# A streamed two-layer decoder trunk: memory transposed as it lands, and a dozen hand-offs in a new order

## The chip, the cores and the metric

One core of one Trainium2 chip. The metric is the device time of one execution in microseconds; less is better. The trace comes from one profiled execution of the same program. The engines are called as in the profile: PE (TensorE), PEld (its weight loads), DVE (VectorE), ACT (ScalarE), POOL (GpSimd) and SP (SyncE, which here only issues DMAs).

## The reference

`x` is 256 tokens by 1024 channels, `mem` 256 rows by 1024, fp32. For each of 2 layers:

```python
h = rms_norm(x);  z = h @ W_in            # one combined projection
x += W_o(sum_i sigmoid(gate_i) * lift_i(branch_i))   # attention, spatial gating, pooling
x += memory_xattn(rms_norm(x), rms_norm(mem))        # 4 heads of 128, 256 memory rows
x += peer_ffn(rms_norm(x))

def memory_xattn(h, mem_h, wq, wk, wv, q_norm, k_norm, wo):
    q = rms_norm((h @ wq) per head, q_norm); k = rms_norm((mem_h @ wk) per head, k_norm)
    p = softmax(q @ k.T * XA_HEAD_DIM ** -0.5);  return (p @ (mem_h @ wv)) @ wo

def peer_ffn(h, wq, keys1, keys2, u_tab, v_tab):     # 8 heads, top 16 of 128*128 experts
    # scores of two half queries against 128 keys each, top 16 of each, top 16 of the 256 sums,
    # softmax weights w;  out = sum over chosen experts e of w_e * gelu(h . u_tab[e]) * v_tab[e]
```

The kernel does not gather experts. It computes gelu(h . U) for all 16384, multiplies by a weight that is zero for those not chosen, and multiplies by the whole of V.

## The kernel before, in words

All weights pass through the core once, as a **stream** of 128x512 pieces in the order in which they are used. A layer has its projection pieces (`PROJ` of them, in the blocks `mem_k, mem_v, z_q ... z_m0-5, lift_*, out0/1, xq, xo0/1, pq0/1`), then 256 pieces of U and 256 of V (two per key, 128 keys). SP loads two pieces per transfer (L427) into a ring `raw` of four. For fp32-like precision each piece is split: ACT writes the rounded part `w_hi` (`hi_piece`, L499), POOL the rest `w_lo = raw - w_hi` (L453), each into one of 4 slots. PE multiplies hi by hi, lo by hi and hi by lo, (`take`, L817 to L819, six 128x512 matmuls a piece; U pieces twelve 128x256 ones, L1079 to L1081; V pieces six, L1108 to L1110) and frees the slot (`used`). ACT's `hi(n)` writes the next n pieces' high parts, 4 ahead of PE; where it stands between ACT's other steps is written by hand, and so is every order in the program: each engine has one instruction list, and `wait(name)`/`step(..., name)` pair them by semaphores. POOL has only the low parts. Products go into 4 PSUM banks `acc` (two blocks of two in turn), transposes and small products into 4 banks `aux`, whose users and order are the table `USES`.

A block's input rows are transposed by PE (L752 memory, L779 all else), read from `aux` by ACT as `h_hi` (L470, L527) and by DVE as `h_lo` (L1171). Products leave through `read_block` on DVE, which scales by 1/rms (L1207).

- **Start.** ACT issues memory, constants, columns and X; SP streams from the beginning. ACT squares the two memory tiles with a sum, takes the root, DVE normalizes them (L1136), PE transposes, ACT and DVE make hi and lo; then the layer loop, whose head is ACT's `hi(SLOTS)`. The same memory preparation for layer 1 lies inside layer 0's V stage (`NORM_AT`, `MEM_AT`).
- **Mixer.** `mix_T0..3` are the transposed rows of the normalized x; ACT writes six pieces' high parts only after `mix_T3`. The attention units (16, each 2 heads) take exponentials on ACT (L601). When `hi` passes the last piece of gate block `z_m{m}`, ACT reads that block at once (`read_gates`, L518), between two units.
- **Memory attention** (L1489 to L1530 on DVE, L636 on ACT, L779, L987, L1007 on PE). The query block is read for both tiles, squared and reduced, then the root. Four units (tile, pair of heads): scores, maximum, exponential, transposes, values, with a ring of two.
- **PEER start.** `ff_T0/1`, eight pieces of pq0, `ff_T2/3`, pq1, then transposes of the queries (`pq_T`) and their 32 score matmuls (L1033), then the U loop over 128 keys.
- **One-hot weights.** During the first half of U, DVE does the top-k (L1577 among it). At key 52 (`EXP_AT`) ACT takes the softmax; at 56 (`SLOTS_AT`) PE transposes the slots; DVE splits them and makes the operands `hot_b` (L1612), `hot_a` (L1620), `hot_w` (L1626) for 8 tokens a step; from key 64 PE multiplies them (L1047, 24 small matmuls) between keys, to the middle of V.
- **V.** PE starts the four `acc` banks with matmuls by zeros, adds all V pieces, closes them by zeros. `eg` is the weighted activation (ACT L696 hi, DVE L1642 lo).
- **Layer end.** DVE adds `acc` to X (L1710), one 128x1024 op per token tile; at the end of the program SP writes X to DRAM in one transfer.

## Time and profile before

| | us |
|---|---|
| median of 3 runs | 2285.96 (2284.37 to 2287.23) |
| the profiled execution's own time | 2284.8 |
| its span in the trace | 2283.0 |
| PE busy | 2194.2 (96%) |
| PEld busy | 1936.4 (85%) |
| POOL busy | 1751.1 (77%) |
| DVE busy | 1400.0 (61%) |
| ACT busy | 1169.1 (51%) |
| streamed | 672 transfers of 512 KB, mean 161 GB/s with all others |

The page gives the chain of work that ended last as 91% PE, 3% DVE, 3% issue, 1% ACT and 1% POOL. In its row of 40 slices PE stands at 9 tenths or more in all but five: the first has 6, the sixth (memory attention and PEER start of layer 0) 7, the slice of the memory attention of layer 1 and one in its U stage have 8, the last 8. A time in a row of the trace counts from the span's start. An idle time in square brackets stands before the group and names what ended it; busy times of matmuls overlap, so that the pitch from start to start is what one costs.

### The profile page before, as it was taken

How to read it: one execution, taken by the hardware profiler on the slowest of the kernel's cores; microseconds unless marked ns; L12 is line 12 of the kernel's file. 1: busy time of each engine (PE TensorE's matmuls, PEld its weight loads, DVE VectorE, ACT ScalarE, POOL GpSimd, SP SyncE). 2: the span in 40 equal slices, each digit the busy share in tenths (PEclk: the TensorE clock that was granted, in tenths of full speed). 3: DMA queues.
4: the chain of work that ended last, by engine and by line, in shares of the span. 5: the costliest groups of instructions: out<-in, count | busy, mean ns of one | idle time of the engine just before them, and what ended most of it. 6: DMA issues, size and time to landing. Idle time of an engine off the chain costs nothing.

```text
span 2283.0 us, 51302 instructions
## 1 busy us (share of the span) xinstructions
PE 2194.2 (96%) x15526; PEld 1936.4 (85%) x15530; DVE 1400.0 (61%) x2291; ACT 1169.1 (51%) x2273; POOL 1751.1 (77%) x1316
## 2 busy tenths in 40 slices
PE   6999979999999999999999998899999999999998
PEld 5887868999999888888878777699999998888887
DVE  4644547994666788734346455489756667886333
ACT  5445654555444455556553555645554444455564
POOL 5745846998777788888885557579987777888886
PEclk9999999999999999999998999999999999999999
DMA  6423423445444444455563234335544444445554
GB/s 243 157 93 110 158 98 136 173 167 182 157 164 157 157 168 169 168 203 187 191 237 130 102 111 166 106 136 174 174 167 164 157 162 159 165 165 191 187 193 147
DMA packets 100517, 367.12 MB, mean 161 GB/s; under 512 B 11472, under 2 KB 11984, under 8 KB 100176
## 3 DMA queue, kind: packets, MB, share of 16 engines
q1 hardware_dynamic: 97040, 353.41, 44.6%
q10 hardware_dynamic: 3392, 12.66, 1.5%
q8 instruction: 42, 0.69, 0.1%
q14 instruction: 43, 0.35, 0.1%
HBM read 364.98 MB, written 1.05 MB: 160 GB/s over the span
## 4 chain that ended last, share of the span: by engine, by line
PE 91%; DVE 3%; issue 3%; ACT 1%; POOL 1%; DVEq 0%; POOLq 0%; ACTq 0%
PE acc L1079 11%; PE acc L1080 10%; PE acc L1081 10%; PE acc L1108 10%; PE acc L1110 10%; PE acc L1109 10%; PE acc L817 6%; PE acc L819 6%; PE acc L818 6%; PE aux L1047 4%; PE aux L779 2%; POOL w_lo L453 1%; PE aux L930 1%; PE aux L865 1%; DVE h_lo L1171 1%
## 5 line engine op out<-in xcount | busy, mean ns | idle before, releaser
L453 POOL TENSOR_TENSOR w_lo<-raw,w_hi 128x512 fp32r<-128x512 f32 x1312 | 1750.9, 1350 | 519.6 <-ACT w_hi L499 424.9
L499 ACT ACTIVATE w_hi<-raw 128x512 fp32r<-128x512 f32 x1344 | 843.3, 630 | 809.3 <-PE acc L1081 424.1
L1079 PE MATMUL acc<-h_hi,w_hi 128*128 128x256 f32 x2048 | 587.0, 287 | 9.7 <-POOL w_lo L453 9.7
L1080 PE MATMUL acc<-h_lo,w_hi 128*128 128x256 f32 x2048 | 579.3, 283 | 0.0
L1081 PE MATMUL acc<-h_hi,w_lo 128*128 128x256 f32 x2048 | 579.0, 283 | 0.0
L1108 PE MATMUL acc<-w_hi,eg 128*128 128x512 f32 x1024 | 406.2, 397 | 1.2 <-DVE eg L1642 1.2
L1079 PEld LDWEIGHTS acc<-h_hi,w_hi 128*128 128x128 f32 x2048 | 392.6, 192 | 12.6 <-POOL w_lo L453 12.5
L1110 PE MATMUL acc<-w_hi,eg 128*128 128x512 f32 x1024 | 399.6, 390 | 0.0
L1109 PE MATMUL acc<-w_lo,eg 128*128 128x512 f32 x1024 | 398.7, 389 | 0.0
L1080 PEld LDWEIGHTS acc<-h_lo,w_hi 128*128 128x128 f32 x2048 | 393.0, 192 | 0.1
L1081 PEld LDWEIGHTS acc<-h_hi,w_lo 128*128 128x128 f32 x2048 | 392.7, 192 | 0.0
L1642 DVE TENSOR_TENSOR eg<-big,eg 128x256 fp32r<-128x256 f32 x256 | 188.5, 736 | 228.7 <-ACT eg L696 227.7
L1612 DVE TENSOR_TENSOR hot_b<-aux,sel 128x1024 bf16<-128x1024 f32 x128 | 156.8, 1225 | 206.4 <-PE aux L1047 186.0
L819 PE MATMUL acc<-w_hi,h_lo 128*128 128x512 f32 x640 | 252.3, 394 | 0.0
L1110 PEld LDWEIGHTS acc<-w_hi,eg 128*128 128x128 f32 x1024 | 192.2, 188 | 41.5
L1108 PEld LDWEIGHTS acc<-w_hi,eg 128*128 128x128 f32 x1024 | 192.4, 188 | 39.7 <-POOL w_lo L453 2.0
L1109 PEld LDWEIGHTS acc<-w_lo,eg 128*128 128x128 f32 x1024 | 192.6, 188 | 38.3
L696 ACT ACTIVATE eg<-big 128x256 fp32r (+1 forms) x256 | 106.8, 418 | 206.3 <-PE acc L1110 206.0
L817 PE MATMUL acc<-w_hi,h_hi 128*128 128x512 f32 x416 | 172.3, 414 | 12.8 <-POOL w_lo L453 5.8
L818 PE MATMUL acc<-w_lo,h_hi 128*128 128x512 f32 x416 | 163.2, 392 | 0.0
L819 PEld LDWEIGHTS acc<-w_hi,h_lo 128*128 128x128 f32 x640 | 121.0, 189 | 26.5
L1626 DVE TENSOR_TENSOR hot_w<-sel,aux 128x1536 bf16<-128x1536 bf16 x64 | 112.3, 1754 | 8.9 <-DVE sel L1620 1.8
(235 smaller groups left out, 2336.8 us busy)
## 6 DMA issues: line engine op xcount, KB each, us to landing
raw<-stream_dram SPq DMA_DIRECT2D x672, 512.0 KB, 3.2
big<-parb_dram ACTq DMA_DIRECT2D x2, 2128.0 KB, 10.1
big<-mem_dram ACTq DMA_DIRECT2D x3, 1024.0 KB, 5.3
big<-pm_dram ACTq DMA_DIRECT2D x2, 768.0 KB, 15.1
big<-parr_dram ACTq DMA_DIRECT2D x2, 640.0 KB, 12.1
X<-x_dram ACTq DMA_DIRECT2D x1, 1024.0 KB, 12.0
out_dram<-X SPq DMA_DIRECT2D x1, 1024.0 KB, 4.0
big<-lnrow_dram ACTq DMA_DIRECT2D x2, 256.0 KB, 13.2
```

Source lines behind the costliest of these rows:

```text
L453: nc.gpsimd.tensor_tensor(w_lo[:, k % SLOTS, :], raw[:, k // PER_CHUNK, k % PER_CHUNK, :], w_hi[:, k % SLOTS, :].bitcast(F32), ALU.subtrac ...
L499: nc.scalar.activation(w_hi[:, k % SLOTS, :], raw[:, (k // PER_CHUNK) % RAW, k % PER_CHUNK, :], ACT.Copy).then_inc(hi_ready, 1)
L817: pe_.matmul(dst, r_hi[:, kt, ts], w_hi[:, slot, :], start=(k == 0), stop=False)
L818: pe_.matmul(dst, r_hi[:, kt, ts], w_lo[:, slot, :], start=False, stop=False)
L819: ins = pe_.matmul(dst, r_lo[:, kt, ts], w_hi[:, slot, :], start=False, stop=(k == depth - 1))
L1079: pe_.matmul(acc[:, q, 0:S], wh, h_hi[:, kt, :], start=(kt == 0), stop=False)
L1080: pe_.matmul(acc[:, q, 0:S], wh, h_lo[:, kt, :], start=False, stop=False)
L1081: ins = pe_.matmul(acc[:, q, 0:S], w_lo[:, r % SLOTS, k * P:(k + 1) * P], h_hi[:, kt, :], start=False, stop=(kt == KD - 1))
L1108: pe_.matmul(dst, eg[:, q % 2, 0, ts], w_hi[:, slot, :], start=False, stop=False)
L1109: pe_.matmul(dst, eg[:, q % 2, 0, ts], w_lo[:, slot, :], start=False, stop=False)
L1110: ins = pe_.matmul(dst, eg[:, q % 2, 1, ts], w_hi[:, slot, :], start=False, stop=False)
L1642: V.tensor_tensor(eg[:, q % 2, 1, :], src, eg[:, q % 2, 0, :].bitcast(F32), ALU.subtract).then_inc(sig["eg_ready"].sem, 1)
```

## The change

- **A, start.** The constants' and memory's transfers go first, and SP holds the stream back until memory, columns and constants have landed. The memory rows are transposed raw; their 1/rms is applied when `mem_k` and `mem_v` are read. DVE takes their squares once per program (`msq`), ACT one root per layer for memory and X together (`factors`). The rows are not normalized in the V stage either. ACT's first four pieces alternate with the memory's high parts.
- **B, mixer.** ACT's squares of X alternate with pieces; `hi(2)` stands ahead of `mix_T3`, `hi(4)` behind.
- **C, gates.** A gate block that comes due within the units is read after the next unit's exponentials.
- **D, memory attention.** Per token tile: rows read by DVE, squares by ACT, reduction by DVE, transposes by PE. The Exp table is asked for ahead of the scores. Rings and banks for all four units; all four score products first.
- **E, PEER start.** `ff_T0..3` at once; keys 0 and 1 of U between the readings of pq0 and pq1, keys 2 and 3 between the queries' transposes and their scores (`first_keys`); the U loop starts at key 4. `EXP_AT, SLOTS_AT` become 56, 60.
- **F, one-hots.** All one-hot operands are bf16 with an innermost pair `[.., 2]`; iota and weight parts lie in PSUM as bf16 pairs, where they were fp32.
- **G, V.** No matmuls by zeros: the first and last pieces carry the start and stop flags. PE does the first two weight steps at the head of V and stays two ahead.
- **H, layer boundary.** ACT writes the next layer's first four high parts at the end of a layer, ahead of its loop branch; SP loads two more chunks at the very end for it.
- **I, layer end.** X is added in half columns, the first half after the last but one piece; output in two transfers, one per token tile.

```diff
+USES += [(f"xs{u}", u) for u in range(len(XUNITS))] + [(f"xp_T{u}", u) for u in range(len(XUNITS))]
+USES += [("xo_0", 0), ("xo_1", 2), ("xo_T0", 1), ("xo_T1", 3)]
 USES += [(f"{r}_T{i}", (i + 2) % 4) for r in ("fu", "ff") for i in range(4)]
-USES += [(f"pq_T{i}", i) for i in range(4)]
...
-EXP_AT, SLOTS_AT = 52, 56
+EXP_AT, SLOTS_AT = 56, 60
...
-        iota_b = sb("iota_b", [P, P], BF16)
+        slot_a = sb("slot_a", [P, S, 2], BF16)
         hot_b = sb("hot_b", [P, G_TOK, KEYS], BF16)
         hot_w0 = sb("hot_w0", [P, G_TOK, PARTS, HALF], BF16)
...
+        xring = region("xring", 2048, 4, 2, MEM)
+        xsquare = region("xring", 1024, T, COL)
+        xpT = region("xpT", 2048, 4, 4, P)
...
-        slots = topv.bitcast(BF16)
-        slot_a, slot_b = slots[:, 0:S], slots[:, S:2 * S]
+        slot_b = topv.bitcast(BF16).rearrange("p (t n) -> p t n", n=2)
         slot_w = sel[:, 512:768]
-        slot_parts = sel[:, 768:1280].bitcast(BF16)[:, 0:PARTS * S].rearrange("p (c t) -> p c t", c=PARTS)
+        slot_parts = hot_w0.rearrange("p t c a -> p (t c a)").rearrange("p (t c n) -> p t c n", c=PARTS, n=2)
...
+        parts_ps = upper[:, 0:PARTS * S].bitcast(BF16).rearrange("p (t c n) -> p t c n", c=PARTS, n=2)
+        rest_ps = upper[:, PARTS * S:PARTS * S + P // 2].bitcast(BF16).rearrange("p (a n) -> p a n", n=2)
...
+            sp.wait_ge(sig["mem_in"].sem, 32)
+            sp.wait_ge(const_in, 16)
...
-            sp.wait_ge(sig["layer_free"].sem, sig["layer_free"].value(DEPTH, 0))
-            sp.dma_start(out.rearrange("(t p) d -> p t d", p=P), X[:]).then_inc(out_done, 16)
-            sp.wait_ge(out_done, 16)
+            for r in range(SLOTS // PER_CHUNK):
+                sp.wait_ge(lo_ready, DEPTH * PIECES + (r + 1) * PER_CHUNK)
+                sp.dma_start(raw[:, r], stream[r:r + 1].rearrange("o p (k c) -> p (o k) c", c=COL)).then_inc(chunk_in[r], 16)
+
+            for t in range(T):
+                sp.wait_ge(sig["layer_free"].sem, sig["layer_free"].value(DEPTH, t - 1))
+                sp.dma_start(out[t * P:(t + 1) * P, :], X[:, t, :]).then_inc(out_done, 16)
+            sp.wait_ge(out_done, T * 16)
...
             for i in range(4):
+                hi_piece(i, 16, i + 1)
                 memory_hi(first, i)
...
+                                due.append(m)
+                                if not late:
+                                    read_gates(due.pop())
...
-                hi(SLOTS)
                 for t in range(T):
                     a.wait("layer_free", t - 1)
                     if t == 0:
                         act.wait_ge(x_in, 16)
                     a.step(nc.scalar.activation(junk[:, t, :], X[:, t, :], ACT.Square, accum_out=ssx[:, t:t + 1]),
                            "x_sq" if t else None)
-                hi(2)
-                root(ssx, "x_mean", "x_sqrt", 1)
+                    hi(1)
+                root(factors, "x_mean", "x_sqrt", 1)
                 hi(1)
...
                 hi_T("mix_T2", 4, 2, C_MIX + 4)
+                hi(2)
                 a.wait_pieces(16)
                 hi_T("mix_T3", 6, 2, C_MIX + 6)
-                hi(6)
+                hi(4)
...
+                    if due:
+                        read_gates(due.pop())
+                    hi(2, u < len(UNITS) - 1)
...
+                    if t == 0:
+                        a.wait("xq_rows")
+                    else:
+                        a.wait_block("xq")
+                    a.step(nc.scalar.activation(xsquare[:, t, :], xqt[:, t, :], ACT.Square), "xq_square")
...
+                a.step(nc.scalar.activation(st[:, 96:97], ident[:, 0:1], ACT.Exp))
...
-                for n in range(2):
-                    hi((3, 8)[n])
-                    for i in (2 * n, 2 * n + 1):
-                        hi_T(f"ff_T{i}", 2 * i, 2, C_FFN + 2 * i)
+                hi(3)
+                for i in range(2):
+                    hi_T(f"ff_T{i}", 2 * i, 2, C_FFN + 2 * i)
+                hi(6)
+                a.wait_pieces(LAST["pq1"] - 2)
+                hi_T("ff_T2", 4, 2, C_FFN + 4)
+                hi(2)
+                a.wait_pieces(LAST["pq1"])
+                hi_T("ff_T3", 6, 2, C_FFN + 6)
                 assert done[0] == PROJ + SLOTS
...
+                hi(SLOTS)
...
+                e.wait_block("mem_v")
+                for u in range(len(XUNITS)):
+                    e.wait_drained(f"xq_T{XUNITS[u][0]}")
+                    xscores(u)
+                xprobs(0)
+                for u in range(len(XUNITS)):
+                    if u + 1 < len(XUNITS):
+                        xprobs(u + 1)
...
+                rows_T([f"ff_T{i}" for i in range(4)], xn)
                 take(8)
...
                 e.wait_block("pq0")
+                first_keys(0)
                 e.wait_block("pq1")
                 rows_T([f"pq_T{i}" for i in range(4)], pq)
+                first_keys(2)
...
+                for k0, k1 in ((4, SLOTS_AT), (SLOTS_AT, HALF), (HALF, KEYS)):
...
-                pe_.wait_ge(zero_set, 1)
-                pe_.wait_ge(sig["u_out"].sem, layer * KEYS + (KEYS + 4))
-                for q in range(4):
-                    pe_.matmul(acc[:, q, :], zeros[:], zeros[:, 0:1].broadcast_to((P, COL)), start=True, stop=False)
...
+                weights_step(0, 0, 1)
+                weights_step(0, 1, 1)
+                for r in range(8):
+                    if r < 2:
+                        pe_.wait_ge(sig["u_out"].sem, layer * KEYS + (KEYS + 3 + r))
+                    value_piece(0, 0, r, start=r < 2)
...
+                            if k0 == 4 and r % 4 == 0:
+                                weights_step(i, r // 4, 1, 2)
...
-            first.step(V.tensor_scalar(ssm, ssm, 1.0 / D, EPS, ALU.mult, ALU.add))
-            dve.sem_inc(mem_mean, 1)
-            dve.wait_ge(mem_sqrt, 1)
-            first.step(V.reciprocal(ssm, ssm))
-            memory_rows(first)
...
+            first.step(V.tensor_tensor(xn, memx, memx, ALU.mult))
+            first.step(V.tensor_reduce(msq, xn, AX.X, ALU.add))
+            first.step(V.tensor_scalar(msq, msq, 1.0 / D, EPS, ALU.mult, ALU.add))
...
-                read_block("mem_k", [(t, 0, COL, mk[:, t, :]) for t in range(T)])
+                read_block("mem_k", [(t, 0, COL, mk[:, t, :]) for t in range(T)], ssm)
...
+                    d.wait("xq_square", t + 1)
+                    d.step(V.tensor_reduce(ssh[:, 4 * t:4 * t + 4], xsquare[:, t, :].rearrange("p (h c) -> p h c", c=XD), AX.X, ALU.add))
+                    if t:
+                        mean(ssh[:, 0:8], XD, "xq_mean")
...
-                    V.tensor_tensor(hot_b[:, :, :], iota_ps.unsqueeze(1).broadcast_to((P, G_TOK, KEYS)),
-                                    tokens(slot_b, i, s).unsqueeze(2).broadcast_to((P, G_TOK, KEYS)),
+                    V.tensor_tensor(hot_b.rearrange("p t (a n) -> p t a n", n=2),
+                                    iota_pairs.unsqueeze(1).broadcast_to((P, G_TOK, KEYS // 2, 2)),
+                                    tokens(slot_b, i, s).unsqueeze(2).broadcast_to((P, G_TOK, KEYS // 2, 2)),
                                     ALU.is_equal).then_inc(sig["hot_b_made"].sem, 1)
...
+                    V.tensor_tensor(hot_w[s % 2].rearrange("p t c (a n) -> p t c a n", n=2),
+                                    hot_a.rearrange("p t (a n) -> p t a n", n=2).unsqueeze(2).broadcast_to(
+                                        (P, G_TOK, PARTS, HALF // 2, 2)),
+                                    parts_ps[:, at, :, :].unsqueeze(3).broadcast_to(
+                                        (P, G_TOK, PARTS, HALF // 2, 2)),
...
-                d.wait("v_out")
-                for t in range(T):
-                    d.step(V.tensor_tensor(X[:, t, :].rearrange("p (n c) -> p n c", n=2),
-                                           X[:, t, :].rearrange("p (n c) -> p n c", n=2),
-                                           acc[:, 2 * t:2 * t + 2, :], ALU.add), "layer_free")
+                for dh in range(2):
+                    d.wait_pieces(PIECES - 1 + dh)
+                    for t in range(T):
+                        v = X[:, t, dh * COL:(dh + 1) * COL]
+                        d.step(V.tensor_tensor(v, v, acc[:, 2 * t + dh, :], ALU.add), "layer_free" if dh else None)
```

**PE at the memory attention** (L779/L800 transposes, L987/L1011 scores, L1007/L1028 values). Before:

```order
L779 MATMUL aux<-cst,big 128x128 x8
L369 REGISTER_ALU
L987 MATMUL aux<-big 128x256 x4
L369 REGISTER_ALU
L779 MATMUL aux<-cst,big 128x128 x4
L987 MATMUL aux<-big 128x256 x2
L369 REGISTER_ALU
L1007 MATMUL aux<-big 128x128 x4
L779 MATMUL aux<-cst,big 128x128 x4
L987 MATMUL aux<-big 128x256 x2
L369 REGISTER_ALU
```

After:

```order
L800 MATMUL aux<-cst,big 128x128 x4
L378 REGISTER_ALU
L800 MATMUL aux<-cst,big 128x128 x4
L367 REGISTER_ALU
L1011 MATMUL aux<-big 128x256 x8
L367 REGISTER_ALU
L800 MATMUL aux<-cst,big 128x128 x8
L367 REGISTER_ALU
L1028 MATMUL aux<-big 128x128 x4
L367 REGISTER_ALU
L800 MATMUL aux<-cst,big 128x128 x4
L1028 MATMUL aux<-big 128x128 x4
```

The query's transposes are now two groups, each with a wait before it; all scores stand ahead of the first transposes of probabilities, and no scores stand between later transposes and values.

**PE from the projections to the keys** (L1079 to L1081 and L1058 to L1060 are the three matmuls of a key; L1033/L1086 the query's scores). Before:

```order
L819 MATMUL acc<-w_hi,h_lo 128x512
L779 MATMUL aux<-cst,big 128x128 x8
L380 REGISTER_ALU x2
L374 REGISTER_ALU
L779 MATMUL aux<-cst,big 128x128 x8
L374 REGISTER_ALU
L779 MATMUL aux<-cst,big 128x128 x4
L374 REGISTER_ALU
L779 MATMUL aux<-cst,big 128x128 x4
L369 REGISTER_ALU x3
L1033 MATMUL aux<-big 128x256 x8
```

After, behind the last matmul of pq1 (the third row below), and the place of the queries' transposes:

```order
L838 MATMUL acc<-w_hi,h_hi 128x512
L839 MATMUL acc<-w_lo,h_hi 128x512
L840 MATMUL acc<-w_hi,h_lo 128x512
L378 REGISTER_ALU
L1066 ISA
L1067 REGISTER_ALU
L367 REGISTER_ALU
L1058 MATMUL acc<-h_hi,w_hi 128x256
L1059 MATMUL acc<-h_lo,w_hi 128x256
L1060 MATMUL acc<-h_hi,w_lo 128x256
```

```order
L1060 MATMUL acc<-h_hi,w_lo 128x256
L378 REGISTER_ALU
L800 MATMUL aux<-cst,big 128x128 x16
L1066 REGISTER_ALU
L1067 REGISTER_ALU
L1058 MATMUL acc<-h_hi,w_hi 128x256
L1059 MATMUL acc<-h_lo,w_hi 128x256
```

Key matmuls now stand ahead of the transposes of the queries, and others between these and the scores.

**ACT around the layer's loop branch** (L499/L489 high part, L696/L716 eg, L547/L552 square of X). Before, the end and then the head:

```order
L695 REGISTER_ALU
L696 ACTIVATE eg<-big 128x256
L499 ACTIVATE w_hi<-raw 128x512
L738 ISA
L487 REGISTER_ALU
L487 COMPARE_AND_BRANCH
```

```order
L498 ISA
L499 ACT_TABLE_LOAD
L499 ACTIVATE w_hi<-raw 128x512
L498 REGISTER_ALU
L499 ACTIVATE w_hi<-raw 128x512
L498 REGISTER_ALU
L499 ACTIVATE w_hi<-raw 128x512
```

After:

```order
L486 REGISTER_ALU
L488 REGISTER_ALU
L489 ACTIVATE w_hi<-raw 128x512
L488 REGISTER_ALU
L489 ACTIVATE w_hi<-raw 128x512
L488 REGISTER_ALU
L489 ACTIVATE w_hi<-raw 128x512
L488 REGISTER_ALU
L489 ACTIVATE w_hi<-raw 128x512
L759 ISA
L498 REGISTER_ALU
L498 COMPARE_AND_BRANCH
```

```order
L498 ISA
L552 ACT_TABLE_LOAD
L552 ACTIVATE big,st<-X 128x1024
L486 ISA
L488 ISA
L489 ACTIVATE w_hi<-raw 128x512
L357 REGISTER_ALU
L552 ACTIVATE big,st<-X 128x1024
```

Four pieces moved from behind the branch to ahead of it, and one stands between the squares.

## Rows read from the trace of the kernel before

**Rows 1.** The page's busy time, span share and instructions of each engine
```profile
PE 2194.2 (96%) x15526; PEld 1936.4 (85%) x15530; DVE 1400.0 (61%) x2291; ACT 1169.1 (51%) x2273; POOL 1751.1 (77%) x1316
```

**Rows 2.** The page's DMA issues: KB each, median us from issue to landing
```profile
raw<-stream_dram SPq DMA_DIRECT2D x672, 512.0 KB, 3.2
...
out_dram<-X SPq DMA_DIRECT2D x1, 1024.0 KB, 4.0
```

**Rows 3.** Timeline of PE at the start: start us, us, engine, line, operation [idle before <-releaser]
```profile
13.45 3.65 PE L752 MATMUL aux<-cst,big 128*128 128x128 f32 x16 [13.45 <-DVE big L1136]
22.32 0.79 PE L817 MATMUL acc<-w_hi,h_hi 128*128 128x512 f32 x1 [5.22 <-POOL w_lo L453]
```

**Rows 4.** Timeline of ACT at the start
```profile
14.57 4.03 ACT L470 ACTIVATE h_hi<-aux,col 128x256 fp32r<-128x256 f32 x8 [3.00 <-PE aux L752]
...
20.21 2.19 ACT L499 ACTIVATE w_hi<-raw 128x512 fp32r<-128x512 f32 x4
```

**Rows 5.** DMA issues of the window 0 to 60 us
```profile
big<-mem_dram ACTq DMA_DIRECT2D x1, 1024.0 KB, 5.6
```

**Rows 6.** Timeline of PE, layer 1, first matmul after mix_T3
```profile
1178.72 0.50 PE L817 MATMUL acc<-w_hi,eg 128*128 128x512 f32 x1 [1.78 <-POOL w_lo L453]
```

**Rows 7.** List of waits: engine line waited for: us in total, times, longest
```profile
PE aux L779 <- ACT big L601: 7.9, 8, 1.4
```

**Rows 8.** Timeline of ACT, reading of a gate block, layer 0
```profile
188.02 1.22 ACT L518 ACTIVATE big<-acc 128x512 f32<-128x512 f32 x2
```

**Rows 9.** Timeline of DVE, memory attention, layer 0
```profile
290.09 1.54 DVE L1207 TENSOR_SCALAR big<-acc,st 128x512 f32<-128x512 f32 x2 [1.66 <-PE acc L819]
291.67 2.14 DVE L1489 TENSOR_TENSOR big<-big 128x1024 f32<-128x1024 f32 x1
293.84 1.22 DVE L1490 TENSOR_REDUCE st<-big 128x8 f32<-128x1024 f32 x1
```

**Rows 10.** Timeline of PE, memory attention, layer 0
```profile
297.19 3.69 PE L987 MATMUL aux<-big 128*128 128x256 f32 x8 [4.41 <-DVE big L1496]
...
312.97 1.09 PE L779 MATMUL aux<-cst,big 128*128 128x128 f32 x8 [0.91 <-DVEq L1527]
```

**Rows 11.** Timeline of ACT, first exponential of memory attention
```profile
300.29 0.56 ACT L636 ACTIVATE big<-aux,st 128x256 f32<-128x256 f32 x1 [3.40 <-DVE st L1508]
...
300.98 0.56 ACT L636 ACTIVATE big<-aux,st 128x256 f32<-128x256 f32 x1
```

**Rows 12.** Timeline of PE between the projections and the keys, layer 0
```profile
355.76 0.66 PE L779 MATMUL aux<-cst,big 128*128 128x128 f32 x4 [1.88 <-DVE h_lo L1171]
...
359.84 7.17 PE L1033 MATMUL aux<-big 128*128 128x256 f32 x32 [1.43 <-DVE big L1540]
```

**Rows 13.** List of waits, as in Rows 7
```profile
PE acc L1108 <- DVE eg L1642: 1.2, 2, 0.6
```

**Rows 14.** Timeline of DVE, top-k, one-hot preparation and first V step, layer 0
```profile
423.93 3.42 DVE L1577 TENSOR_TENSOR big<-sel,ranks 128x4096 bf16<-128x4096 bf16 x1
...
535.55 0.69 DVE L1594 CAST sel<-aux 128x512 bf16<-128x512 f32 x1 [6.59 <-PE aux L779]
...
545.75 1.75 DVE L1626 TENSOR_TENSOR hot_w<-sel,aux 128x1536 bf16<-128x1536 bf16 x1
...
771.08 1.23 DVE L1612 TENSOR_TENSOR hot_b<-aux,sel 128x1024 bf16<-128x1024 f32 x1 [0.61 <-PE aux L1047]
```

**Rows 15.** Timeline of PE, first one-hot product, layer 0
```profile
558.53 0.87 PE L1047 MATMUL aux<-hot_w,hot_b 128*128 128x64 bf16 x24
```

**Rows 16.** Timeline of POOL beside the top-k
```profile
423.91 13.22 POOL L453 TENSOR_TENSOR w_lo<-raw,w_hi 128x512 fp32r<-128x512 f32 x6
```

**Rows 17.** Timeline of ACT at the end of layer 0
```profile
1146.74 1.28 ACT L499 ACT_TABLE_LOAD   x1 [2.94 <-issue]
```

**Rows 18.** Timeline of PE at the start of layer 1
```profile
1151.20 0.49 PE L817 MATMUL acc<-w_hi,h_hi 128*128 128x512 f32 x1 [2.05 <-DVE X L1710]
```

**Rows 19.** Timeline of DVE at the end
```profile
2276.08 2.48 DVE L1710 TENSOR_TENSOR X<-X,acc 128x1024 f32<-128x1024 f32 x2 [4.19 <-PE acc L1113]
```

269 lines of the change are left out of this document (130 added, 139 removed).

## The prediction

> **What bounds the kernel now.** I read the page first: PE is busy 96% of the span, POOL 77% [rows 1]. Nothing in the change takes a weight piece away from PE, so what can be won is PE's idle time, a handful of auxiliary matmuls, and the two ends at which PE has nothing to do. Next the list of waits and the timeline of PE: each idle stretch of PE is a hand-off between engines at a change of stage. They are the start, until the first piece's matmul at 22.32 [rows 3]; one after `mix_T3` [rows 6]; those behind the reading of gates [rows 7]; the memory attention, from 290.09 to 312.97 [rows 9, 10]; the queries before the keys [rows 12]; the start and middle of V [rows 13, 14]; the layer boundary [rows 17, 18]; and the end [rows 19, 2]. In the two long loops PE has no wait worth naming, so a cost that the change puts there counts only if a cover is used up. All terms are for both layers unless said.
>
> **A, start: -7.5.** PE could not transpose memory until 13.45, since ACT and DVE first normalized it; high parts of memory (4.03 for eight) and then four pieces (2.19) came one after the other on ACT [rows 3, 4]. Now PE needs only the landed rows. The memory transfer takes 5.6 in a window shared with the stream [rows 5], and with about 2 for issue it is there at 7.6. The stream starts then, its first chunk lands 3.2 later [rows 2], a high part takes 0.55 (2.19 / 4), a low part 1.33 (1751.1 / 1316) [rows 1]: 12.7 instead of 22.32, so -9.6. Ready transposes and their eight readings (4.03) lie beside it. I give 2.1 back, as ACT's squares of X, a table load of 1.28 [rows 17] and a root now come when PE is already on the pieces and eats its lead of four slots. Bounds: -4 (X, 1 MB behind the constants, late) and -10.
>
> **B: -3.6.** After `mix_T3` PE waits 1.78 for POOL, whose high part stood behind `hi_T` on ACT [rows 6]. Two pieces now stand ahead: 2 x 1.78. Bounds 0 and -3.6. The squares alternating with pieces cost nothing as long as the first piece is written before PE is there.
>
> **C, gates: -4.2.** Eight waits of the transposes for the exponentials sum to 7.9 [rows 7]; they come when ACT reads a gate block (1.22) [rows 8] between scores and exponentials. Three of four readings a layer move behind; the fourth stays (1.4 each, the longest) [rows 7]. 7.9 - 2 x 1.4 = 5.1, less 0.9 for the later piece that now waits for the reading instead. The cover is the ring of four slots, 4 x 1.4 ahead. Bounds -2 and -5.1.
>
> **D, memory attention: -13.** Before, from the reading of xq at 290.09 (two of 0.77) come the square over both tiles (2.14), the reduction (1.22), mean, root and the scaling of transposes, and PE starts scores at 297.19, after 4.41 of idle time [rows 9, 10]. Now the first tile is read at 290.9; ACT squares it (0.61 for a 128x512) [rows 8], DVE reduces it (0.61, half of 1.22) and scales its transposes (0.77), and PE's first scores can start at about 293.3; DVE's first reduction also no longer waits for the square of both tiles. That is -3.9. From the first score to the first exponential 3.1 passed (300.29 - 297.19), from there to the transposes of `xo` 12.7 for eight exponentials at a pitch of 0.69 [rows 10, 11], where 8 x 0.69 = 5.5 would do: the rest is the ring of two, in which scores, copy and values take turns. With four of everything the last exponential ends at 293.3 + 3.1 + 5.5 = 301.9, and transposes, copy, values and the scaling of the last tile need some 3.5 to 4.1 more: 305.4 to 306. Against 312.97 that is 7 to 7.5; I take 6.5, because idle PE has come with the lower of the two clock levels here and PE's first pieces afterwards may run at it. 2 x 6.5. Bounds -10 and -17.
>
> **E, PEER start: -6.6.** 1.88 before the first transposes of queries and 1.43 before their scores [rows 12]; keys 0 to 3 fill both. 2 x 3.31. The 32 score matmuls (7.17) stay. Behind this nothing is removed: eight U pieces only move. `EXP_AT` and `SLOTS_AT` move four keys later, so one-hot preparation has 8 pieces of PE instead of 16. Before, it had 558.53 - 535.55 = 23.0 [rows 14, 15], so now 11.5. It took 545.75 + 1.75 - 535.55 = 11.95. The paired copies and the iota in PSUM add about 1.25, the three one-hot operands at half their time (1.23, 1.75 and the small one) save about 1.85: 11.35, which just fits. At full time it is 13.2, and PE stalls 1.8. Bounds 0 and +3.6; I take 0, since the one packed comparison in the trace runs at 0.84 ns an element against 1.14 for the unpacked `hot_w` [rows 14]. A rule speaks against it: the Trainium skill, page "VectorE: DVE Perf Modes", section "The perf-mode tier table", keeps tensor_tensor with any PSUM operand at its slowest mode; by it this term would be +3.6, and no row shows a packed operand in PSUM.
>
> **F, one-hots: 0 in the loop.** `hot_b` costs 1.2 ns an element, `hot_w` 1.14 (1754 ns for 1536), the packed comparison of the top-k 0.84 (3.42 for 4096) [rows 14]. DVE is busy 61% in all and is not waited for in the loop, so faster one-hots have only idle time to win. Low parts on POOL take 2.2 each beside the top-k (13.22 for six) against 1.33 on the mean [rows 16, 1]; whether the new form does that is the third rival.
>
> **G, V: -1.2 +1.0.** No normalized rows in the middle of V: the two waits behind them sum to 1.2 [rows 13]. At V's head PE now makes two weight steps before the first piece, and the second needs `hot_rows` of DVE, which stand behind the first `eg` low part; the comparable op ran 1.23 after a 0.61 wait [rows 14]. I take 0.5 a layer, bounds 0 and 1.1.
>
> **H, boundary: +1.0** (there is one). ACT jumped back early, its 2.94 of issue time hidden behind PE's last pieces, and its table load began at 1146.74 [rows 17]. Now its last four high parts wait for the last pieces of V, the jump comes after them, some 5 later, and then the table load (1.28) and a square stand ahead of the fifth piece: The closing matmuls by zeros are four of 512 columns, 0.9 at six for 1.4; V's last piece ended at 1151.20 - 2.05 - 0.9 = 1148.3 [rows 18]. So: 1148.3 + 0.55 + 2.94 + 1.28 + 1.2 for a square = 1154.3, the fifth high part; with a low part it is ready at 1156.2. PE, from about 1150.5, has four pieces ready (to 1156.1), so the fifth comes just in time, but a second square and the root with its own table load (1.28) stand ahead of the sixth and seventh: some 1.9 of stall, of which the 0.9 of the zeros comes off. Bounds -1 and +3.
>
> **I, end: -3.0.** The zeros (0.9) go; of the additions, 2 x 1.24 [rows 19], half runs beside the last piece; and the last transfer is 512 KB (3.2 for such a one) [rows 2] against 1 MB in 4.0: -0.9 -1.2 -0.8 = -2.9, rounded up. Bounds -1.5 and -4.5.
>
> **Sum:** -7.5 -3.6 -4.2 -13 -6.6 -1.2 +1.0 +1.0 -3.0 = -37.1. The profiled execution took 2284.8, so 2247.7; the median stands 1.2 above it, so **2249**. All lower bounds together give -49 (2237), all upper ones -9 (2277); they will not all fall on one side.
>
> **Rivals.**
> (1) *PSUM operands keep the one-hots at full time.* The operands iota and parts are in PSUM, before and after; the 0.84 ns is for operands both in SBUF, the 1.14 for one in PSUM [rows 14]. Then the preparation needs 13.2 in 11.5, PE stalls about 1.8, and the head of V 0.6 more: 2 x 2.4 = +4.8, **2254**. The rule of the Trainium skill's page "VectorE: DVE Perf Modes" cited under E says this; the section "Why PSUM operands drop a tier" of that page leaves bf16 the half time. Chance 0.22.
> (2) *Half of what the hand-offs lose returns.* PE reaches the next stage earlier, and there meets POOL or ACT, which are not earlier: POOL's low part is what ended those waits [rows 3, 6]. Half of B to E (27.4) is 13.7, and the start 4 less: 2249 + 17.7 = **2267**. For it: pieces are read 4 ahead, no more. Against it: ACT and POOL are idle in the same stretches. Chance 0.14.
> (3) *Slower: the paired one-hots take POOL's access to SBUF.* While such an op runs, a low part takes 2.2 rather than 1.33 [rows 16]. The one-hots last 1.85 for four pieces, so POOL loses 1.85 x (1 - 1.33 / 2.2) = 0.73. PE needs 5.75 for four U pieces (23.0 / 4), POOL 5.33: 0.42 of slack, from which point on POOL decides. 0.31 over it, in 128 such steps, is +40: **2289**. For it: the top-k's comparison, the one packed form in the trace, is where POOL slows. Against it: its operands are both in SBUF, here one is in PSUM. The Trainium skill, page "GPSIMD Engine Reference", section "Key points", names contention with DVE instructions of two SBUF inputs or in a two-port mode; by that this rival needs the two-port mode. Chance 0.04.
> (4) *Nothing moves*, as the waits are other than read: 2285. Chance 0.02.
>
> **How the numbers follow.** Forecast 0.58, rivals 0.22, 0.14, 0.04, 0.02. A measurement of this kernel can tell about 0.2% from no change, 4.6 us. Faster: 0.58 + 0.22 + 0.14 = 0.94; same 0.02; slower 0.04. The forecast's own range is 2237 to 2261 (the bounds of A, D and H are most of it). The range is 2236 (all lower bounds, and 1 for the spread of runs) to 2264: it takes in rival 1 and not quite half of rival 2.
>
> **What would show it.** In the trace after: PE's first piece near 12.7; no wait behind `mix_T3`; two waits for L607 instead of eight; `xo` transposes 16 after the reading of xq instead of 23; scores of the queries directly behind keys; first one-hot product not waiting for DVE (waiting: rival 1); a low part of POOL at 1.3 in the second half of U (2: rival 3); PE idle between the fourth and eighth piece of layer 1; the last addition of 0.7 and 3.2 to the end. I am wrong if XA gives under 4 a layer, if POOL's mean rises, or if PE waits at new places for over 10 in all.

## The result and the profile after

| us | before | changed |
|---|---|---|
| median | 2285.16 (4 runs, 2282.68 to 2287.23) | 2246.42 (4 runs, 2245.05 to 2247.14) |
| span of the profiled execution | 2283.0 | 2244.7 |
| PE busy | 2194.2 (96%) | 2190.7 (98%) |
| DVE busy | 1400.0 | 1182.9 |

The ratio is 0.983, 95% interval 0.9813 to 0.9847: faster by 38.7, or 1.7% (the forecast was 2249, that is -37.1). From the page of the changed kernel (busy times; two groups; one row of DMA issues), to be read beside [rows 1, 2]:

```profile
PE 2190.7 (98%) x15514; PEld 1936.3 (86%) x15514; DVE 1182.9 (53%) x2295; ACT 1169.5 (52%) x2277; POOL 1742.0 (78%) x1316
...
L458 POOL TENSOR_TENSOR w_lo<-raw,w_hi 128x512 fp32r<-128x512 f32 x1312 | 1741.8, 1342 | 493.1 <-ACT w_hi L489 385.2
...
L1660 DVE TENSOR_TENSOR hot_b<-aux,sel 128x1024 bf16<-128x1024 bf16 x128 | 88.5, 691 | 377.4 <-PE aux L1100 377.3
...
out_dram<-X SPq DMA_DIRECT2D x2, 512.0 KB, 2.9
```

PE's busy time fell by only 3.5; the gain is idle time of PE that is gone. To see where, I numbered the stream's pieces in the order in which PE takes them and subtracted, piece by piece, the start of its first matmul in the changed kernel's trace from that in the trace of before. The lead grows or shrinks only at a few pieces:

```
                                        layer 0   layer 1   both    forecast
A  first piece 22.32 -> 13.05             +9.3
   lost again on mem_k 3 to mem_v 6       -3.6                +5.7     +7.5
B  z_q 1 to 6, behind mix_T3              +2.2      +2.2      +4.4     +3.6
C  z_m3, z_m4, z_m5 (second piece)        +3.0      +2.9      +5.9     +4.2
D  reading of xq to first piece of xo     +7.2      +7.0     +14.2    +13.0
E  pq1 to key 4 (its second piece)        +3.8      +3.8      +7.5     +6.6
   one-hot preparation, keys 55 to 64     -1.1      -1.1      -2.1      0
G  head of V                              -0.4      -0.4      -0.8     -1.0
   middle of V (key 76)                   +0.9      +0.9      +1.8     +1.2
H  first piece of layer 1                           +1.7
   lost again on pieces 4 to 7 of mem_k             -2.9      -1.2     -1.0
I  last piece to the end of the span                          +2.7     +3.0
sum                                                          +38.1    +37.1
```

The places add up to the difference of the spans, 38.3, to within 0.2. Two kinds of loss stand in both kernels, move by some pieces and cancel: stretches in the mixer in which PE's granted clock is 0.5, the lower of its two levels (17.1 a layer in either trace), and two waits of 2.7 to 2.8 a layer in the first half of U, beside the top-k (run 3).

The list of waits (us in total, times, longest); [rows 7] had 7.9 in eight waits for the gates' exponentials:

```profile
PEld aux L800 <- ACT big L607: 5.8, 10, 1.8
...
PE aux L800 <- ACT big L607: 2.7, 2, 1.3
...
PE aux L1100 <- DVE hot_w L1677: 1.8, 2, 0.9
```

PE itself waits for those exponentials twice, 2.7 in all; the larger sum is that of its weight loads (PEld), which was 11.6 in 14 waits before.

The start of PE, then of ACT (start us, us, engine line operation [idle before <-releaser]), beside [rows 3, 4]:

```profile
7.13 3.65 PE L773 MATMUL aux<-cst,big 128*128 128x128 f32 x16 [7.13 <-DVEq L1174]
13.05 0.79 PE L838 MATMUL acc<-w_hi,h_hi 128*128 128x512 f32 x1 [2.27 <-DVE h_lo L1183]
```

```profile
10.46 0.63 ACT L489 ACTIVATE w_hi<-raw 128x512 fp32r<-128x512 f32 x1 [6.23 <-DMA raw<-stream_dram]
11.00 0.96 ACT L475 ACTIVATE h_hi<-aux,col 128x256 fp32r<-128x256 f32 x2
...
16.85 1.28 ACT L552 ACT_TABLE_LOAD   x1 [0.29 <-ACT h_hi L475]
18.14 1.06 ACT L552 ACTIVATE big<-X 128x1024 f32<-128x1024 f32 x1
...
21.92 1.28 ACT L545 ACT_TABLE_LOAD   x1
```

The transposes begin at 7.13 instead of 13.45, and pieces alternate with memory's high parts. Then the two squares, and two table loads (1.28 each) where one was foreseen, stand between ACT and the fifth to eighth piece, while PE, 9.3 earlier than before, uses up the four it has. The seventh piece stands behind the root, and the root waits for something else again: DVE's squares, reduction and scaling of the raw memory rows, which part A puts there (DVE, then ACT's root):

```profile
17.70 2.29 DVE L1195 TENSOR_TENSOR big<-big 128x2048 f32<-128x2048 f32 x1
20.02 2.29 DVE L1196 TENSOR_REDUCE st<-big 128x2 f32<-128x2048 f32 x1
22.34 0.96 DVE L1197 TENSOR_SCALAR st<-st 128x2 f32<-128x2 f32 x1
```

```profile
24.03 0.20 ACT L545 ACTIVATE st<-st 128x4 f32<-128x4 f32 x1 [0.83 <-DVE st L1228]
```

Memory attention of layer 0: DVE, ACT and PE, beside [rows 9 to 11]:

```profile
279.20 1.54 DVE L1525 TENSOR_SCALAR big<-acc,st 128x512 f32<-128x512 f32 x2 [1.66 <-PE acc L840]
```

```profile
283.49 1.28 ACT L647 ACT_TABLE_LOAD   x1
...
285.46 0.56 ACT L651 ACTIVATE big<-aux,st 128x256 f32<-128x256 f32 x1 [0.48 <-DVE st L1546]
...
290.53 0.56 ACT L651 ACTIVATE big<-aux,st 128x256 f32<-128x256 f32 x1
```

```profile
282.39 5.24 PE L1011 MATMUL aux<-big 128*128 128x256 f32 x16 [0.94 <-DVE big L1534]
...
294.94 1.09 PE L800 MATMUL aux<-cst,big 128*128 128x128 f32 x8 [0.91 <-DVEq L1568]
```

From the reading of xq to the first scores pass 3.2 (282.39 - 279.20), where it was 7.1. The Exp table is loaded right behind the root, as it was before, where ACT then idled 3.4 [rows 11]: asking for it early won nothing. The eight exponentials run at a pitch of 0.7 to 290.53 without a hole, and `xo` is transposed at 294.94, 15.7 after the reading. It had been 22.9.

DVE's one-hot preparation in layer 0, beside [rows 14]:

```profile
525.21 0.69 DVE L1637 CAST slot_a<-aux 128x512 bf16<-128x512 f32 x1 [6.58 <-PE aux L800]
...
527.12 0.97 DVE L1643 CAST hot_w<-sel 128x512 bf16<-128x512 f32 x1
528.13 1.49 DVE L1645 TENSOR_TENSOR sel<-sel,hot_w 128x256 f32<-128x256 f32 x1
...
535.59 0.69 DVE L1660 TENSOR_TENSOR hot_b<-aux,sel 128x1024 bf16<-128x1024 bf16 x1
536.20 0.41 DVE L1669 TENSOR_TENSOR sel<-aux,slot_a 128x512 bf16<-128x512 bf16 x1
536.65 0.95 DVE L1677 TENSOR_TENSOR hot_w<-sel,aux 128x1536 bf16<-128x1536 bf16 x1
```

It lasts from 525.21 to 537.60, 12.4, and PE waits for it (0.9, twice, in the list above). The one-hots took about the half, with an operand in PSUM: 0.69 for 1.22, 0.41 for 0.68, 0.95 for 1.75. But the casts into pairs (L1643) take 0.97, 1.42 and 1.42, and the two subtractions (L1645) 1.49 each. In the kernel before, the same five took 0.31, 1.27 and 1.27, and 1.40 each; two of them:

```profile
537.09 1.40 DVE L1601 TENSOR_TENSOR sel<-sel 128x256 f32<-128x256 f32 x1
538.52 1.27 DVE L1599 CAST sel<-sel 128x256 bf16<-128x256 f32 x1
```

The layer boundary, ACT and PE, and DVE at the end, beside [rows 17 to 19]:

```profile
1126.85 0.63 ACT L489 ACTIVATE w_hi<-raw 128x512 fp32r<-128x512 f32 x1 [0.72 <-PE acc L1143]
1130.09 1.28 ACT L552 ACT_TABLE_LOAD   x1 [2.61 <-issue]
1131.39 1.06 ACT L552 ACTIVATE big<-X 128x1024 f32<-128x1024 f32 x1
```

```profile
1128.05 0.49 PE L838 MATMUL acc<-w_hi,h_hi 128*128 128x512 f32 x1 [1.23 <-DVE X L1763]
...
1134.84 0.49 PE L838 MATMUL acc<-w_hi,h_hi 128*128 128x512 f32 x1 [1.06 <-POOL w_lo L458]
...
1139.01 0.50 PE L838 MATMUL acc<-w_hi,h_hi 128*128 128x512 f32 x1 [0.78 <-POOL w_lo L458]
```

```profile
2238.11 2.94 DVE L1763 TENSOR_TENSOR X<-X,acc 128x512 f32<-128x512 f32 x4 [1.91 <-PE acc L1143]
```

PE's first piece comes 1.2 after the last of V (2.05 in rows 18), the fifth waits 1.06 and the seventh 0.78 for low parts. The four half additions take 2.94, 0.74 each, and two of them lie beside the last piece.

### The profile page after: what moved, and what is told of

The parts are those of the page before. It is cut to its first block, busy times and chain, and to the rows that moved or that the text cites. A ratio compares the mean times of both kernels' runs of the same rounds, so it can differ in the third digit from the quotient of the medians.

```text
span 2244.7 us, 51285 instructions
## 1 busy us (share of the span) xinstructions
PE 2190.7 (98%) x15514; PEld 1936.3 (86%) x15514; DVE 1182.9 (53%) x2295; ACT 1169.5 (52%) x2277; POOL 1742.0 (78%) x1316
## 4 chain that ended last, share of the span: by engine, by line
PE 92%; issue 3%; DVE 3%; POOL 1%; ACT 1%; POOLq 0%; DVEq 0%
PE acc L1058 11%; PE acc L1141 11%; PE acc L1143 10%; PE acc L1142 10%; PE acc L1059 10%; PE acc L1060 10%; PE acc L838 6%; PE acc L840 6%; PE acc L839 6%; PE aux L1100 4%; PE aux L800 2%; POOL w_lo L458 1%; PE aux L951 1%; PE aux L974 1%; PE aux L886 1%
## 5 line engine op out<-in xcount | busy, mean ns | idle before, releaser
L489 ACT ACTIVATE w_hi<-raw 128x512 fp32r<-128x512 f32 x1348 | 845.3, 629 | 807.8 <-PE acc L1060 419.6
L1058 PE MATMUL acc<-h_hi,w_hi 128*128 128x256 f32 x2048 | 587.3, 287 | 10.6 <-POOL w_lo L458 9.6
L1060 PE MATMUL acc<-h_hi,w_lo 128*128 128x256 f32 x2048 | 579.1, 283 | 0.0
L1058 PEld LDWEIGHTS acc<-h_hi,w_hi 128*128 128x128 f32 x2048 | 392.6, 192 | 14.1 <-POOL w_lo L458 12.5
L1060 PEld LDWEIGHTS acc<-h_hi,w_lo 128*128 128x128 f32 x2048 | 392.7, 192 | 0.0
L1695 DVE TENSOR_TENSOR eg<-big,eg 128x256 fp32r<-128x256 f32 x256 | 175.2, 685 | 248.7 <-ACT eg L716 242.7
L1660 DVE TENSOR_TENSOR hot_b<-aux,sel 128x1024 bf16<-128x1024 bf16 x128 | 88.5, 691 | 377.4 <-PE aux L1100 377.3
L1142 PEld LDWEIGHTS acc<-w_lo,eg 128*128 128x128 f32 x1024 | 192.6, 188 | 38.3
L716 ACT ACTIVATE eg<-big 128x256 fp32r (+1 forms) x256 | 106.8, 418 | 203.8 <-PE acc L1143 203.5
L838 PE MATMUL acc<-w_hi,h_hi 128*128 128x512 f32 x416 | 173.5, 417 | 12.4 <-DVE h_lo L1207 4.8
L838 PEld LDWEIGHTS acc<-w_hi,h_hi 128*128 128x128 f32 x416 | 78.9, 190 | 36.2 <-issue 9.5
## 6 DMA issues: line engine op xcount, KB each, us to landing
big<-parr_dram ACTq DMA_DIRECT2D x2, 640.0 KB, 12.7
```

The source lines that it names most:

```text
L489: nc.scalar.activation(w_hi[:, k % SLOTS, :], raw[:, (k // PER_CHUNK) % RAW, k % PER_CHUNK, :], ACT.Copy).then_inc(hi_ready, 1)
L838: pe_.matmul(dst, r_hi[:, kt, ts], w_hi[:, slot, :], start=(k == 0), stop=False)
L1058: pe_.matmul(dst, wh, h_hi[:, kt, :], start=(kt == 0), stop=False)
L1060: return pe_.matmul(dst, w_lo[:, r % SLOTS, wk * P:(wk + 1) * P], h_hi[:, kt, :], start=False, stop=(kt == KD - 1))
L1142: pe_.matmul(dst, eg[:, q % 2, 0, ts], w_lo[:, slot, :], start=False, stop=False)
L1695: V.tensor_tensor(eg[:, q % 2, 1, :], src, eg[:, q % 2, 0, :].bitcast(F32), ALU.subtract).then_inc(sig["eg_ready"].sem, 1)
```

## The experiments

Each is the changed kernel with one edit, unless said, and each but the last was executed once. One execution in total moves by up to 5 for reasons that are in no edit: at the pieces z_m0 and z_m1, which no experiment touched, the lead moves by 0, 1.6 or 3.3 a layer, as stretches at the lower clock there are shorter in one trace than in another, and by 4.9 over both layers in run 3. The first piece starts between 12.9 and 14.3 (without runs 6 and 11, which move it). So I read each at its place, as the change of PE's lead over the changed kernel there. No run takes back B, G, I or the raw transposes of A: for these the table above is the evidence.

**1. The preparation's operands.** `rest_w` is the bank in which the transposes left the weights; `slot_w` and its copy go.

```diff
-                d.step(V.tensor_copy(slot_w, bank("slot_T1")[:, 0:S]), drains="slot_T1")
+                rest_w = bank("slot_T1")[:, 0:S]
...
-                        d.step(V.tensor_tensor(slot_w, slot_w, slot_parts[:, :, c, 0], ALU.subtract))
+                        d.step(V.tensor_tensor(rest_w, rest_w, slot_parts[:, :, c, 0], ALU.subtract))
```

> The changed kernel with the splitting of the slot weights done in PSUM (the rest of the weights stays in the bank in which the transposes left it, one copy goes). In the changed kernel PE loses 1.1 at key 64 of each layer, waiting for DVE's one-hot preparation, which takes 12.4. Theory (SBUF ports): two subtractions of 128x256 take 1.49 and two casts 1.42 where the same shape takes 0.43 and 0.97 elsewhere, because DVE waits for POOL's low part when it wants both SBUF inputs or its fast mode; with one operand in PSUM the four lose about 0.9 each, preparation falls to 8.5 or less, PE's 1.1 go: 2.2 over both layers. Rival (the pair layout itself is slow): only the copy of 0.42 goes, preparation stays near 12, PE still loses 0.7: 0.8 in all.

Measured: at key 64 PE is 1.06 and 1.07 earlier, the stall is gone in both layers. Preparation lasts 8.9 (526.30 to 535.16). The same cast and subtraction now, on DVE:

```profile
527.75 0.69 DVE L1643 CAST hot_w<-aux 128x512 bf16<-128x512 f32 x1
528.48 0.50 DVE L1646 TENSOR_TENSOR aux<-aux,hot_w 128x256 f32<-128x256 f32 x1
```

So most of a cast's or subtraction's time here was a wait for SBUF, not the pair layout. But the kernel before shows the same long casts and subtractions (1.27 and 1.40), so the wait is not what made the preparation longer than the forecast; the section on the prediction takes that apart. The execution took 2249.0 all the same: at the head of V the granted clock was at the lower level for 3.4 in both layers, which cost 1.6 each and did not happen in the changed kernel's trace.

**2. One-hots with both inputs in SBUF.**

```diff
+        iota_b = sb("iota_b", [P, KEYS // 2, 2], BF16)
...
-                iota_pairs = rest_ps
+                iota_pairs = iota_b[:, :, :]
```

> The changed kernel with the iota operand of hot_b and hot_a in SBUF instead of PSUM, so that both comparisons have two SBUF inputs. This is the forecast's third rival made real. Theory (DVE is the one that waits): hot_b goes from 0.69 to about 1.6 and hot_a from 0.41 to about 1.3, POOL's low part stays at 1.3, PE has no new wait, time within 3 of the changed kernel (2246). Rival (POOL is the one that waits): POOL's low parts go to 1.6 or more in the second half of U, PE waits for them, time at least 2260, up to 2290.

Measured: 2256.0. The groups `hot_b` and `hot_a` (xcount | busy, mean ns | idle before):

```profile
L1662 DVE TENSOR_TENSOR hot_b<-iota_b,sel 128x1024 bf16<-128x1024 bf16 x128 | 155.7, 1217 | 248.5 <-PE aux L1101 248.4
L1671 DVE TENSOR_TENSOR sel<-iota_b,slot_a 128x512 bf16<-128x512 bf16 x128 | 123.2, 962 | 0.1
```

`hot_b` takes 1217 ns instead of 691, `hot_a` 962 instead of 414. In layer 0 the low part stays at 1.29 in the second half of U; in the first half of V it is 1.42 instead of 1.29, 57 of 127 above 1.5. PE loses 4.5 at key 64 in either layer, where the preparation's own comparisons now wait and the clock falls to its lower level for 3.4, 1.6 at the head of V in layer 0 (the clock again) and 0.4 a layer in the loop of V. The theory is right for who waits: DVE, nearly always; the time it gave (within 3) is wrong, since I left out that the preparation is on PE's path. The third rival's place (the loops) does not give way even then.

**3. The top-k's operands.** The largest packed operations of DVE, only for the second token tile.

```diff
+                    if t:
...
+                        d.step(V.tensor_scalar(aux[:, 2, 128:256].bitcast(U32), topf[:, 0:128].bitcast(U32), 0, None,
+                                               ALU.bitwise_or))
+                        rk, found = (aux[:, 2, at:at + 128].bitcast(BF16).rearrange("p (f j h) -> p f j h", f=2, j=TOPK)
+                                     for at in (0, 128))
...
-                                           ranks.unsqueeze(3).broadcast_to((P, 2, 16, 16, PH)), ALU.is_equal))
+                                           rk.unsqueeze(3).broadcast_to((P, 2, 16, 16, PH)), ALU.is_equal))
```

> The changed kernel with the ranks and the found indices of the second token tile's top-k comparison copied to a free PSUM bank, so that the 128x4096 comparison and product have one SBUF input; the first tile's stay as they are and serve as the control. PE loses 2.5 near U piece 46 (first tile) and 2.5 near piece 97 (second tile) in either kernel, waiting for low parts of POOL that take 2 to 3 there. Theory (two SBUF inputs of DVE slow POOL): the low parts beside the second tile's two large operations stay near 1.3, PE's loss at piece 97 falls to 1 or less, the one at 46 stays 2.5; 3 to 4 in all over both layers. Rival (it is the length of the operations or the packed mode, wherever the operands lie): both stay 2.5.

Measured: at pieces 103 to 105 of U the lead grows by 2.7 in either layer; at 44 to 54, the control, by nothing. The execution took 2236.8; 5.4 of its 9.7 are at this place, and most of the rest is at z_m0 and z_m1. DVE's comparison and product (the comparison 3.42 in [rows 14], the product 3.27):

```profile
489.57 2.29 DVE L1628 TENSOR_TENSOR big<-sel,aux 128x4096 bf16<-128x4096 bf16 x1
491.90 2.29 DVE L1632 TENSOR_TENSOR big<-big,aux 128x4096 bf16<-128x4096 bf16 x1
```

POOL in the same window, in this kernel and in the changed one:

```profile
487.46 19.22 POOL L458 TENSOR_TENSOR w_lo<-raw,w_hi 128x512 fp32r<-128x512 f32 x13
```

```profile
486.94 20.30 POOL L458 TENSOR_TENSOR w_lo<-raw,w_hi 128x512 fp32r<-128x512 f32 x11
```

Thirteen low parts in 19.2 against eleven in 20.3. This is the largest wait of PE that both kernels have in the loops, and my prediction had passed over it ("no wait worth naming"), although the list of waits had PE waiting for low parts at the U matmuls, 9.7 in ten waits before and 9.6 now.

**4. One table load less.** Ahead of the squares of X:

```diff
+                a.step(nc.scalar.activation(st[:, 96:97], ident[:, 0:1], ACT.Sqrt))
```

> The changed kernel with a dummy square root of one element ahead of the squares of X at the head of each layer. In the changed kernel ACT loads a table for the squares and another for the root (1.28 each), and PE loses 3.0 in layer 0 and 2.9 in layer 1 on pieces 4 to 7 of mem_k. Theory: the squares and copies run with the root's table, one load of 1.28 goes, and pieces 6 and 7 come up to 1.3 earlier in both layers: 2 to 2.5 less. Rival: each function asks for a table of its own, loads stay two or become three: 0 to +1.

Measured: 2246.4, no gain. ACT at the boundary shows that the load is gone (one, then root, squares and copies without another):

```profile
1129.04 1.28 ACT L548 ACT_TABLE_LOAD   x1 [2.24 <-issue]
```

Piece 6 of mem_k comes 0.7 earlier in layer 1, but pieces 4 to 7 of mem_v give 0.9 back. In layer 0 PE loses from the first piece to mem_v 6 what it lost before, 3.5. There the load was hidden: the root, which waited 0.83 for DVE behind its load of 1.28, now waits for DVE all of it.

```profile
25.55 0.20 ACT L545 ACTIVATE st<-st 128x4 f32<-128x4 f32 x1 [2.12 <-DVE st L1229]
```

(This execution began its first piece 1.2 later than the changed kernel's, so 25.55 stands beside 24.03.)

**5. Part C undone.**

```diff
-                    hi(2, u < len(UNITS) - 1)
+                    hi(2)
```

> The changed kernel with part C undone alone: ACT reads a gate block as soon as it comes due within the units. Theory (each reading stands between scores and exponentials, and PE waits for it): slower by 4.2 (the forecast's term) to 5.9 (what the two traces show between z_m2 and z_m5 of both layers), all of it in the stretches behind the first pieces of z_m3, z_m4 and z_m5. Rival (the forecast's second: what a hand-off gains is given back a little later): the loss at those pieces is made up before the layer ends, less than 3 in all.

Measured: 2252.2. The lead falls by 0.57, 1.33 and 1.11 at the second pieces of z_m3, z_m4 and z_m5 in either layer, 0.1 less in all by the end of z_m5: 5.9 together, and none of it comes back. The list of waits has its eight waits of 7.9 again. The second rival is refuted at this place.

**6. Part H undone** (and SP's two more chunks).

```diff
             for i in range(4):
-                hi_piece(i, 16, i + 1)
                 memory_hi(first, i)
...
-                done = [SLOTS]
+                done = [0]
...
+                hi(SLOTS)
                 for t in range(T):
                     a.wait("layer_free", t - 1)
...
                 assert key == KEYS and done[0] == PIECES
-                hi(SLOTS)
```

> The changed kernel with part H undone: the next layer's first four high parts stand behind ACT's loop branch again (and so, in layer 0, behind all of memory's high parts, which undoes that piece of part A). Theory: in the changed kernel H costs 1 net at the boundary, since ACT's jump, table load and square come in the open after its last four pieces and PE loses 2.9 on pieces 4 to 7; with H undone this 2.9 goes and the first piece of layer 1 comes 1 to 1.5 later: 1 to 2 less at the boundary. At the start of layer 0 the four pieces come later: 1 to 2 more there. Rival (PE's own jump sets the start of layer 1 and the table loads follow in any case): pieces 4 to 7 lose the same 2.9, boundary 1 or more slower.

Measured: 2242.7. ACT and PE at the boundary:

```profile
1125.64 1.28 ACT L485 ACT_TABLE_LOAD   x1 [3.16 <-issue]
1126.94 2.19 ACT L485 ACTIVATE w_hi<-raw 128x512 fp32r<-128x512 f32 x4
```

```profile
1129.05 0.49 PE L833 MATMUL acc<-w_hi,h_hi 128*128 128x512 f32 x1 [2.11 <-POOL w_lo L454]
```

The first piece is 0.9 later, pieces 4 to 7 are not late (+2.9): 2.0 better at the boundary. At the start of layer 0 the first piece is 3.8 later (16.85), and by mem_v 6 nothing is left of that. So H costs 2.0, and alternating ACT's first four pieces with memory's high parts is worth 0: what was 3.8 earlier waits at the fifth to seventh piece.

**7. Part E without its cover.**

```diff
                 e.wait_block("pq0")
-                first_keys(0)
                 e.wait_block("pq1")
                 rows_T([f"pq_T{i}" for i in range(4)], pq)
-                first_keys(2)
...
+                first_keys(0)
+                first_keys(2)
```

> The changed kernel with keys 0 to 3 behind the scores of the queries on PE, as the whole U loop stood before; the order of all other engines stays. Theory (the keys fill PE's waits for the reading of pq1, for the transposes' copies and for the scores): slower by 3.3 to 4.0 a layer, 6.6 to 8 in all, with three waits of 0.5 to 1.9 back on PE between pq1 and the keys. Rival (the keys only change places with waits that come anyway, such as POOL's lead after the scores): less than 3.

Measured: 2258.6; 6.6 lost by key 4 in either layer, of which some 1.6 each is a stretch of 3.4 at the lower clock (the 16 transposes below take 3.49, in the changed kernel 1.91). PE in layer 0:

```profile
338.53 3.49 PE L800 MATMUL aux<-cst,big 128*128 128x128 f32 x16 [4.37 <-DVE big L1243]
342.97 7.14 PE L1084 MATMUL aux<-big 128*128 128x256 f32 x32 [0.95 <-DVE big L1581]
```

The waits are 4.4 and 1.0, not the 1.88 and 1.43 of [rows 12]: with `ff_T0` to `ff_T3` ahead of it, DVE reads pq1 later than before. More than the theory's 3.3 to 4.0 is lost. The new order needs the keys.

**8. V's second weight step behind two pieces.**

```diff
-                weights_step(0, 1, 1)
                 for r in range(8):
+                    if r == 2:
+                        weights_step(0, 1, 1)
```

> The changed kernel with the second weight step of V behind the first two pieces instead of ahead of them. In the changed kernel PE idles 2.28 between the two weight steps, waiting for DVE's operands, while the first key's eg is ready 1.4 before the first piece starts. Theory: the first piece of V comes 1.3 to 1.5 earlier, the weight step (0.7) is done two pieces later without a wait: 2.6 to 3.0 less over both layers. Rival (eg or the freeing of the banks holds the first piece): 0.

Measured: 2242.0, but only 0.4 at the third piece of V and 0.3 from the fourth on, in either layer (the first piece is 1.2 earlier, the third has 0.7 less than that). PE in this kernel, then in the changed one:

```profile
748.41 0.49 PE L1141 MATMUL acc<-w_hi,eg 128*128 128x512 f32 x1 [1.81 <-DVE eg L1696]
```

```profile
750.38 0.86 PE L1100 MATMUL aux<-sel,hot_b 128*128 128x64 bf16 x24 [2.28 <-issue]
```

The first piece comes nearly as much earlier as the theory said. But PE still idles 1.81 behind the first weight step, now for eg, where it idled 2.28 for the one-hots, and the second step (0.7) has only changed places: the theory counted its time as won.

**9. Scores in turn.**

```diff
-                    xscores(u)
+                    if u < 2:
+                        xscores(u)
                 xprobs(0)
+                xscores(2)
                 for u in range(len(XUNITS)):
                     if u + 1 < len(XUNITS):
                         xprobs(u + 1)
+                    if u == 0:
+                        xscores(3)
                     xvalues(u)
```

> The changed kernel with PE's scores of the third and fourth unit of memory attention in turn with the first transposes of probabilities and values, as a ring of two would have them; banks and rings stay four. Part D gains 7.1 a layer in the traces (from the reading of xq to the first piece of xo). Theory (the forecast's split: some 4 from the earlier first scores, some 3 from all scores first): the exponentials of units 3 and 4 wait for their scores, 2 to 3.5 a layer slower, 4 to 7 in all. Rival (ACT's exponentials at a pitch of 0.7 are slower than anything PE does, the order is without weight, and all 7.1 come from the earlier start): within 1.

Measured: 1.3 a layer at the first piece of xo (1.35 and 1.29), less than I expected and more than the rival. ACT waits once for a maximum:

```profile
287.50 0.56 ACT L651 ACTIVATE big<-aux,st 128x256 f32<-128x256 f32 x1 [1.21 <-DVE st L1550]
```

Of D's 7.1, the order of scores is 1.3; 3.9 is the earlier first score (3.2 for 7.1), and the other 1.9 are the rest of the ring of two, which no run took apart.

**10. The stream not held back.**

```diff
-            sp.wait_ge(sig["mem_in"].sem, 32)
-            sp.wait_ge(const_in, 16)
```

> The changed kernel with SP's stream not held back until memory, columns and constants have landed. Theory (they share the DMA engines): memory lands 1 to 3 later, so do PE's transposes (7.1 now) and its first piece (13.1 now): 1 to 3 slower at the start, of which half may be made up since the chunks are there earlier. Rival (ACT's alternation of pieces and high parts sets the first piece, and the chunk's landing at 10.4 starts it): the first piece comes 1 to 2 earlier.

Measured: 2247.8, first piece at 13.10 for 13.05, the lead at mem_v 6 the same. Both were wrong about the first piece. PE's transposes do start 2.7 later, when the columns have landed:

```profile
9.80 3.60 PE L771 MATMUL aux<-cst,big 128*128 128x128 f32 x16 [9.80 <-DMA col<-cols_dram]
```

But ACT writes the first high part at 7.35 instead of 10.46, and its first high part of memory comes at 10.92 instead of 11.00. The two effects cancel: holding back the stream moves PE's first piece by nothing.

**11. Four edits together**, for both tiles of the top-k: 1, 3 (for the first tile one bank of scores is copied to SBUF ahead), 6, and DVE's second comparison of V ahead of the first key's low part.

```diff
+                held = region("w1", 4096)[:, 2560:3072]
...
+                    if t == 0:
+                        d.wait_filled("ps1_2")
+                        d.step(V.tensor_copy(held, bank("ps1_2")), drains="ps1_2")
...
+                hot_rows(0, 1, 1)
                 d.wait("g_out", G_STEPS)
                 weighted(0, 0)
```

> The changed kernel with four edits at once: ranks and found indices of both token tiles' top-k in PSUM (one score bank of the second tile is copied to SBUF early to free it), the splitting of slot weights in PSUM, DVE's second one-hot comparison of V ahead of the first key's low part, and part H undone. By the traces: four stalls of 2.5 at the top-k (10), two of 1.1 at key 64 (2.1), 0.5 to 1 twice at the head of V (1 to 2), 2 to 2.5 at the boundary: 15 to 17 less than 2246.4, so 2230 (2227 to 2235). Rival (POOL or ACT is the next bound in the same places): half of it, 2238.

Measured: 2226.78 (5 runs, 2226.09 to 2229.24), ratio to before 0.9747, interval 0.9734 to 0.976; 20 less than the changed kernel. PE's busy time:

```profile
PE 2181.3 (98%) x15514; PEld 1932.4 (87%) x15514; DVE 1167.4 (52%) x2303; ACT 1166.7 (52%) x2273; POOL 1726.8 (78%) x1316
```

At the places: four stalls of the top-k 2.7 to 2.8 each (11.0), key 64 1.1 twice, V's head 1.1 twice, the boundary 0.6 (with a stretch at the lower clock that run 6 did not have). That is 16, within the 15 to 17 expected; some 3 more, in the mixer's low stretches of the traced execution, are in no edit, and they put the median just below the expected range (2227 to 2235).

## Why the prediction was right, and where it was not

- **The sum** came out, -37.1 against -38.7, and no rival did: eight of ten terms lie within 1.7 of what the traces show. It is closer than its terms, though, and that is luck: six are under by 5.4 in all, four over by 4.4. The views that carried it were PE's idle groups at changes of stage with their releasers. All upper bounds together give about -17, not the -9 of the prediction; the stated range does not hang on that.
- **A** was over-sized: the first piece came as forecast (12.7; 13.05), but 3.6, not 2.1, were given back. The step that failed is the list behind the squares. It had one table load and one root; there were two loads, and the root also waits for DVE's squares of the raw memory (17.70 to 23.30), a wait that the prediction put at nothing. Run 4 took one load away, and the root then waited 2.12 for DVE instead of 1.28 and 0.83. No run moved DVE's squares, so what they cost is open.
- **B, C, D, E** were each under-sized by 0.8 to 1.7. In C I had subtracted 0.9 for a piece that waits in place of the gates; run 5 gives 5.9 for C, with no such loss. In E a third idle of PE was left out, 0.47: 1.88, 0.47 and 1.43 make the 3.8 a layer that was measured. The row of the kernel before that was passed over:

```profile
356.88 1.53 PE L779 MATMUL aux<-cst,big 128*128 128x128 f32 x12 [0.47 <-DVE h_lo L1171]
```

- **Preparation** is the step that went wrong: 11.35 forecast, 12.4 measured, 11.5 available, and PE loses 1.1 in each layer, 2.1 in all. "Paired copies and the iota add about 1.25" was 2.0: a cast more for `slot_b` (0.7), 1.0 in the three casts, 0.2 each in the subtractions and the iota. And the one-hots saved 1.6, not 1.85. The wait for POOL, which run 1 removes together with the stall, is no part of this difference: by its rows the kernel before had it as well.
- **One-hots at half time** came true (691 ns for 1225, 955 for 1754), but the rows named for it did not say so: 0.84 against 1.14 ns an element is three quarters. And the 0.84 was of an operation with both inputs in SBUF beside a busy POOL; with one input in PSUM it ran at 0.56 (run 3).
- **"No wait worth naming"** in the two long loops was wrong: beside the top-k PE waits four times, 11 in all (runs 3 and 11). It did not touch the sum, since both kernels have it.
- **The first rival** (one-hots at full time with an operand in PSUM) did not happen. The Trainium skill, page "VectorE: DVE Perf Modes", section "The perf-mode tier table", would have had the one-hots unchanged; the trace does not agree, and agrees with its section "Why PSUM operands drop a tier".
- **The second rival** (refunds) happened at A and H, where a whole engine's list was shifted, and at none of the hand-offs B to E.
- **The third** did not happen; run 2 shows that with two SBUF inputs DVE would be the one to wait, all but 0.4 a layer.
- **H** came out as forecast (-1.0; -1.2) by luck: its parts were +1.7 and -2.9, where +0.9 and -1.9 were foreseen. Run 6 shows a loss of 2.0 inside the gain.

## What to carry to other kernels

On a kernel whose busiest engine stands at 96%, subtract the starts of the same work item in two traces: the lead changes at a dozen places only, and each is a term to be checked by itself, far below what total times can tell. A wait removed by order alone (read the gates after the next exponentials) stays removed; what a list of work moved to an earlier place on the same engine gained was given back here, at the start and at the boundary, as soon as that engine's other work was late. Where one engine streams from SBUF all the time, ask of each operation of the other where its inputs lie.

## What the runs showed of the hardware

- DVE and POOL share SBUF at a price on both sides: a 128x256 operation on two inputs in SBUF took 0.43 with POOL idle (the product ahead of the preparation) and 1.49 with it busy, and 0.50 with one operand in PSUM and POOL busy; a 128x4096 comparison 3.42 against 2.29. POOL's low part took up to 3.3 beside the long ones, 1.3 else. The Trainium skill, page "GPSIMD Engine Reference", section "Key points", names the contention for two SBUF inputs; the trace agrees, and the runs add that DVE's short operations pay 0.7 to 1.1 each (a cast 1.42 against 0.69 from PSUM).
- Packed bf16 pairs with one operand in PSUM ran at 0.56 to 0.68 ns an element (2.29 for 4096, 0.69 for 1024).
- Short idle stretches of PE at a change of stage were followed by 3.4 at the lower clock level (granted clock 0.5, that is 1.2 GHz) in some executions and not in others (head of V: runs 1, 2, 5, 6, 10, not the changed kernel's own trace), 1.4 to 1.6 each. I had counted it only for memory attention.
